# Where a per-head normalisation is computed: moving the retention norm from GpSimd to VectorE, with its square root made by Newton steps, and a weight panel split in quarters

## The reference

```python
def retention(rq, rk, rv, rg, cos, sin):
    ...  # o: per head, (q k^T * decay) v with causal exponential decay
    mu = jnp.mean(o, axis=-1, keepdims=True)
    var = jnp.mean(jnp.square(o - mu), axis=-1, keepdims=True)
    o = ((o - mu) * lax.rsqrt(var + GROUPNORM_EPS)).reshape(B, S, H * DV)
    return (o * jax.nn.silu(rg.astype(jnp.float32))).astype(rq.dtype)

for l in range(DEPTH_2):
    ...
    a = mla_attention(...)          # 8 heads, softmax attention
    r = retention(...)              # 8 heads
    mixed = jnp.concatenate([rmsnorm_2(a, beta_attn[l]), r * beta_ret[l]], axis=-1)
    x = x + mixed @ w_o[l]
    h = rmsnorm_2(x, mlp_norm[l])
    x = x + jnp.square(jax.nn.relu(h @ w_up[l])) @ w_down[l]
```

## Time and profile before

| what | us |
|---|---|
| median of 3 runs | 3416.02 |
| lowest and highest of the 3 | 3414.8 and 3417.39 |
| the profiled execution's own time | 3417.14 |
| its span | 3415.2 |
| PE busy in the span | 3308.8 |
| DVE, ACT, POOL busy | 1870.1, 1443.7, 323.3 |

### The profile page before, as it was taken

One profiled execution on the slowest core, in us unless ns is written; L12 is line 12 of the kernel. 1 busy time (PEld: TensorE's weight loads), 2 busy tenths in 40 slices (PEclk: granted clock), 3 DMA queues, 4 the chain that ended last, 5 costly groups with the idle time before them and its releaser, 6 DMA issues.

```text
span 3415.2 us, 45463 instructions
## 1 busy us (share of the span) xinstructions
PE 3308.8 (97%) x17167; PEld 2818.1 (83%) x17167; DVE 1870.1 (55%) x1978; ACT 1443.7 (42%) x1539; POOL 323.3 (9%) x272
## 2 busy tenths in 40 slices
PE   6999999999999899999999999999998999999998
PEld 6988788888888788778888888878877888888886
DVE  5877565555444544655555544454465555554444
ACT  5335453344344443544433444443354444334343
POOL 5332010000000101510000000000052000000000
PEclk9999999999999999999999999999999999999999
DMA  6444556555555455435665555555543555655553
GB/s 189 148 126 149 185 180 188 184 184 194 189 195 196 148 191 175 134 111 177 190 187 184 186 195 196 189 181 187 182 144 99 185 186 185 192 187 193 189 195 135
DMA packets 216948, 598.48 MB, mean 175 GB/s; under 512 B 16136, under 2 KB 57320, under 8 KB 183032
## 3 DMA queue, kind: packets, MB, share of 16 engines
q1 hardware_dynamic: 215528, 589.58, 53.0%
q0 software_dynamic: 1312, 7.41, 0.6%
HBM read 594.86 MB, written 2.10 MB: 175 GB/s over the span
## 4 chain that ended last, share of the span: by engine, by line
PE 90%; DVE 4%; issue 2%; ACT 2%; POOL 1%; DVEq 1%; POOLq 1%; ACTq 0%
PE ps L511 43%; PE ps L576 21%; PE ps L580 10%; PE ps L1137 5%; PE ps L926 3%; DVE wlo L1792 2%; PE ps L647 1%; PE ps L648 1%; PE ps L649 1%; ACT whi L1207 1%; PE ps L1076 0%; PE ps L1077 0%; PE ps L541 0%; PE ps L1106 0%; DVEq L1856 0%
## 5 line engine op out<-in xcount | busy, mean ns | idle before, releaser
L1792 DVE TENSOR_TENSOR wlo<-raw,whi 128x2048 fp32r<-128x2048 f32 (+2 forms) x547 | 1254.5, 2293 | 1277.3 <-ACT whi L1207 1276.2
L1207 ACT CAST whi<-raw 128x2048 fp32r<-128x2048 f32 (+2 forms) x552 | 1034.4, 1874 | 1530.8 <-PE ps L511 869.7
L576 PE MATMUL ps<-xT,whi 128*128 128x512 f32 x3072 | 840.2, 395 | 0.9 <-DVE xT L1818 0.9
L511 PE MATMUL ps<-whi,stage 128*128 128x512 f32 x3168 | 785.4, 389 | 2.9 <-DVE wlo L1792 2.4
L511 PEld LDWEIGHTS ps<-whi,stage 128*128 128x128 f32 x3168 | 594.1, 188 | 127.9 <-DVE wlo L1792 3.9
L576 PEld LDWEIGHTS ps<-xT,whi 128*128 128x128 f32 x3072 | 525.5, 189 | 72.2 <-DVE xT L1818 1.4
L580 PEld LDWEIGHTS ps<-xT,wlo 128*128 128x128 f32 x3072 | 472.1, 189 | 65.7
L580 PE MATMUL ps<-xT,wlo 128*128 128x256 f32 x3072 | 489.1, 281 | 0.0
L511 PE MATMUL ps<-wlo,stage 128*128 128x512 f32 x1584 | 424.1, 389 | 0.0
L511 PEld LDWEIGHTS ps<-wlo,stage 128*128 128x128 f32 x1584 | 297.4, 188 | 61.7
L511 PE MATMUL ps<-whi,xT 128*128 128x512 f32 x1344 | 336.3, 385 | 11.5 <-DVE wlo L1792 6.5
(11 more groups left out here) (423 smaller groups left out, 2401.9 us busy)
## 6 DMA issues: line engine op xcount, KB each, us to landing
raw<-in_mlp_w SPq DMA_DIRECT2D x128, 1024.0 KB, 5.1
raw<-in_w_up SPq DMA_DIRECT2D x128, 1024.0 KB, 5.3
raw<-in_w_down SPq DMA_DIRECT2D x128, 1024.0 KB, 4.9
raw<-in_w_in SPq DMA_DIRECT2D x100, 1024.0 KB, 5.2
raw<-in_w_o SPq DMA_DIRECT2D x32, 1024.0 KB, 5.2
raw<-in_w_out SPq DMA_DIRECT2D x16, 1024.0 KB, 5.2
raw<-in_w_in SPq DMA_DIRECT2D x16, 832.0 KB, 4.5
raw<-in_w_uq SPq DMA_DIRECT2D x8, 768.0 KB, 4.2
```

What stands on the lines that cost most here:

```text
L511: last = mm(psum(bank, width), x_of(part, r), w[:, s, at + c0:at + c0 + width], start=start and part == 0 and w is whi, stop=stop and part ...
L576: mm(psum(bank + j), whi[:, u % 2, c:c + P], xT[:, k, :], start=k == 0, stop=False)
L1207: act.copy(whi[:, u % 2, 0:width], raw[:, u, 0:width]).then_inc(sig["hi"], 1)
L1792: tt(wlo[:, u % 2, 0:width], raw[:, u, 0:width], whi[:, u % 2, 0:width].bitcast(F32), SUB).then_inc(sig["lo"], 1)
```

## The change

ACT no longer makes the root: DVE computes it at step 10 (`inverse_roots`) from an integer seed and three Newton steps, 12 small instructions with a drain between each two. DVE then normalises one pair of heads per step at steps 11 to 14 (`normalise`), in four instructions of 128 x 128. POOL waits for each pair (`nrm`) and only gates. The transposes of the pairs, their high parts and their low parts come one step later. The decays of heads 0 and 1 are made ahead, between the Silu and the cast of w_ukv's first panel. The cast of w_o's panel 0 becomes four parts of 512 columns at ACT's steps 2 to 5, its split four parts at DVE's steps 6 to 9; the cast of panel 1 four parts at ACT's steps 14 to 17. DVE's split of panel 1 moves from step 15 to step 18 and that of panel 2 from step 19 to step 20, both whole.

```diff
 PE, steps
-                    if 12 <= step < 16:
-                        retention_transposes(step - 12)
+                    if 13 <= step < 17:
+                        retention_transposes(step - 13)
 ACT, helper
+            def split_part(Q, u, c):
+                if c == 0:
+                    act.wait_ge(sig[f"raw{u}"], 16 * (Q + 1))
+                    act.wait_ge(sig["pan"], 4 * Q + u - 1)
+                part = act.copy(whi[:, u % 2, 512 * c:512 * c + 512], raw[:, u, 512 * c:512 * c + 512])
+                if c == 3:
+                    part.then_inc(sig["hi"], 1)
 ACT, behind the Silu
+                decays(0)
+                decays(1)
 ACT, steps
-                    if 1 <= step < 9:
+                    if 3 <= step < 9:
                         decays(step - 1)
                     if 2 <= step < 10:
                         retention_out(step - 2)
-                    if step == 5:
-                        split(w_o["quad"], 0, D)
-                    if step == 10:
-                        act.wait_ge(sig["gn"], at["gn"] + 1)
-                        fn(gstat[:, 2, :], moments[:, :, 1], ACT.Sqrt, bias=eps).then_inc(sig["gsq"], 1)
-                    if 13 <= step < 17:
-                        retention_hi(step - 13)
+                    if 2 <= step < 6:
+                        split_part(w_o["quad"], 0, step - 2)
+                    if 14 <= step < 18:
+                        retention_hi(step - 14)
                     if 10 <= step < 18:
                         softmax(step - 2)
-                    if step == 14:
-                        split(w_o["quad"], 1, D)
+                    if 14 <= step < 18:
+                        split_part(w_o["quad"], 1, step - 14)
 DVE, new
+                def inverse_roots():
+                    v, t, y = gstat[:, 0, :], gstat[:, 1, :], gstat[:, 2, :]
+                    ts(v, moments[:, :, 1], EPS, None, ADD)
+                    dve.drain()
+                    ts(y.bitcast(I32), v.bitcast(I32), 1, None, ALU.logical_shift_right)
+                    dve.drain()
+                    ts(y.bitcast(I32), y.bitcast(I32), -1, ROOT_SEED, MUL, ADD)
+                    for _ in range(3):
+                        dve.drain()
+                        tt(t, y, y, MUL)
+                        dve.drain()
+                        stt(t, t, -0.5, v, MUL, MUL)
+                        dve.drain()
+                        stt(y, t, 1.5, y, ADD, MUL)
+                    dve.drain()
+                def normalise(p):
+                    for h in (2 * p, 2 * p + 1):
+                        for r in range(RT):
+                            y, i = proj[:, r, C_RQ + h * P:C_RQ + (h + 1) * P], 8 * r + h
+                            last = ts(y, y, moments[:, i, 0:1], gstat[:, 2, i:i + 1], SUB, MUL)
+                    last.then_inc(sig["nrm"], 1)
 DVE, steps
-                        moments_of(7).then_inc(sig["gn"], 1)
+                        moments_of(7)
                     if 1 <= step < 17:
                         scores(step - 1)
                     if 3 <= step < 10:
                         moments_of(step - 3)
-                    if step == 6:
-                        split(w_o["quad"], 0, D)
+                    if 6 <= step < 10:
+                        split_part(w_o["quad"], 0, step - 6)
                     if step == 10:
-                        dve.wait_ge(sig["gsq"], at["gsq"] + 1)
-                        dve.reciprocal(gstat[:, 2, :], gstat[:, 2, :]).then_inc(sig["grc"], 1)
+                        inverse_roots()
+                    if 11 <= step < 15:
+                        normalise(step - 11)
                     if 11 <= step < 19:
                         weights(step - 3)
-                    if 13 <= step < 17:
-                        retention_lo(step - 13)
-                    if step == 15:
+                    if 14 <= step < 18:
+                        retention_lo(step - 14)
+                    if step == 18:
                         split(w_o["quad"], 1, D)
-                    if step == 19:
+                    if step == 20:
                         split(w_o["quad"], 2, D)
 POOL
-                    pool.wait_ge(sig["grc"], heads["grc"] + 1)
-                    ...
                     for p in range(4):
-                        ...
-                        pool.drain()
+                        pool.wait_ge(sig["nrm"], heads["nrm"] + p + 1)
                         c = slice(C_RQ + 2 * p * P, C_RQ + 2 * (p + 1) * P)
                         g = slice(C_RG + 2 * p * P, C_RG + 2 * (p + 1) * P)
                         tt(proj[:, :, c], proj[:, :, c], proj[:, :, g], MUL).then_inc(sig["ret"], 1)
```

More of the change, by code:

```diff
@@ L42 @@
 ROUND = 1.5 * 2.0 ** 23
+ROOT_SEED = 0x5f3759df
 W_IN1 = 4620
@@ L121 @@
     heads=dict(tT=16, evT=16, sc=16, wr=8, dS=16, nb=8, pr=8, xp=8, pt=8, vv=16, oo=8, om=8,
-               gn=1, gsq=1, grc=1, ret=4, rtr=4, rhi=4, rlo=4),
+               nrm=4, ret=4, rtr=4, rhi=4, rlo=4),
     mixed=dict(mx=1, mla=1, tr=4, trhi=4, xt=4), w_o=dict(quad=4),
@@ L333, in build @@
                  "evD", "evT", "fe", "fin", "fl", "fmix", "fn", "fp", "fsc", "ft", "fv", "fx", "g1", "g2",
-                 "g3", "g4", "g5", "gel", "gn", "gsh", "gst", "hi", "hn", "ld_cst", "ld_dt", "dtr", "ld_gain", "ld_gb",
+                 "g3", "g4", "g5", "gel", "nrm", "gsh", "gst", "hi", "hn", "ld_cst", "ld_dt", "dtr", "ld_gain", "ld_gb",
                  "ld_pos", "ld_pw", "ld_rows", "ld_ssm", "ld_x", "ld_xm", "ld_xr", "lo", "mix", "mlx", "msc", "g3f", "fxs", "fxl", "pxs", "pxl", "sxs", "sxl", "mxs", "mxl",
@@ L338, in build @@
                  "tT", "tr", "trhi", "upd", "uph", "vev", "vtr", "vv", "om", "rtr", "rhi", "rlo", "wm", "wr", "xn", "xp",
-                 "xt", "gsq", "grc", "ret", "mla", "half", "rsr", "tile", "sq", "ssum", "yps", "yst", "yt", "prm_c", "s5rot", "yev", "ld_x1", "ld_cst2", "evG", "ld_rows2", "zeros", "cpy2", "rawh0", "rawh1", "rawh2", "rawh3", "xmn", "mo0", "resid0", "zb", "zs"]
+                 "xt", "ret", "mla", "half", "rsr", "tile", "sq", "ssum", "yps", "yst", "yt", "prm_c", "s5rot", "yev", "ld_x1", "ld_cst2", "evG", "ld_rows2", "zeros", "cpy2", "rawh0", "rawh1", "rawh2", "rawh3", "xmn", "mo0", "resid0", "zb", "zs"]
         sig = {n: ctx.enter_context(nc.semaphore(n)) for n in names}
@@ L1648, in _, with decays @@
                     fn(proj[:, r, C_RG:W_IN2], proj[:, r, C_RG:W_IN2], ACT.Silu)
+                at = st.peek("heads")
+                def decays(i):
+                    if i >= 2:
+                        act.wait_ge(sig["dS"], at["dS"] + i - 1)
+                    fn(decay[:, i % 2, :], const("rel"), ACT.Exp, scale=LOG_GAMMA[i]).then_inc(sig["wr"], 1)
+                decays(0)
+                decays(1)
                 def q_rows():
@@ L1682, in transposed @@
                     last.then_inc(sig["evT"], 1)
[L1684 to L1687, removed]
                 def softmax(i):
@@ L1787, in _, with split_part @@
             MUL, ADD, SUB = ALU.mult, ALU.add, ALU.subtract
+            def split_part(Q, u, c):
+                if c == 0:
+                    dve.wait_ge(sig["hi"], 4 * Q + u + 1)
+                columns = slice(512 * c, 512 * c + 512)
+                part = tt(wlo[:, u % 2, columns], raw[:, u, columns], whi[:, u % 2, columns].bitcast(F32), SUB)
+                if c == 3:
+                    part.then_inc(sig["lo"], 1)
             def split(Q, u, width):
@@ L2457, in moments_of @@
                     for r in range(RT):
-                        last = dve.bn_aggr(moments[:, 8 * r + h, :], stats6[:, r, :])
+                        dve.bn_aggr(moments[:, 8 * r + h, :], stats6[:, r, :])
                     dve.drain()
-                    return last
+                def inverse_roots():
[19 more added lines that the diff above has]
+                    last.then_inc(sig["nrm"], 1)
                 def retention_lo(p):
@@ L2743, in _ @@
                     last.then_inc(sig["rope"], 1)
-                    pool.wait_ge(sig["grc"], heads["grc"] + 1)
-                    for r in range(RT):
-                        y = proj[:, r, C_RQ:C_RQ + 2 * P].rearrange("p (h n) -> p h n", h=2)
-                        tt(y, y, moments[:, 8 * r:8 * r + 2, 0:1].to_broadcast([P, 2, P]), SUB)
-                    pool.drain()
-                    for p in range(4):
[L2752 to L2759, removed]
+                    for p in range(4):
+                        pool.wait_ge(sig["nrm"], heads["nrm"] + p + 1)
                         c = slice(C_RQ + 2 * p * P, C_RQ + 2 * (p + 1) * P)
```

## The result

The changed kernel takes 3422.94 us (median of 20 runs, 3418.64 to 3427.64) against 3415.64 for the kernel before (20 runs, 3412.91 to 3417.54): ratio 1.0022, 95% interval 1.0015 to 1.0029. It is slower by 7.3 us; the interval does not hold 1. The profiled execution took 3419.29, span 3417.5, the third fastest of the twenty; the profiled execution of before took 3417.14. So the two traces differ by 2.15 us only, and not by 7.3.

The account below looks back on a forecast made before the run. PE, busy 97% of the span, bounds the kernel; its heads-stage gaps end on DVE and ACT. Per layer -6.85 + 2.5 + 0.3 + 5.1 = +1.05, so 3419.2 for one execution, median 3418.1; predicted 3418, range 3408.5 to 3424.

Parts of the forecast that it names:

- little changes: Forecast case: two to four slow-clock stretches in a layer, 3413.9 to 3419.9 us; chance 0.57.
- POOL's work bound nothing: Heads stage: no long PE gap ends on POOL, 8.4 us of slack, so moving the norm wins nothing by itself.
- Decays ahead, -0.15: Before w_ukv's first panel PE loses 0.85; before head 0's values 1.0 comes back; net -0.15 us.
- Quarters, -2.5 in a layer: Retention steps: PE's stalls on panel 0's whole cast and whole split go, gaining 1.0 + 1.5 us.
- Normalisation, 0.75 for a pair: DVE steps 11 to 14: 0.19 us per 128x128 operation from SBUF, 0.75 for a pair (0.36 to 1.2).
- DVE's walk to item 8's weights: DVE's scores, moments, root and pair 0 put the weights at 50.3; PE's gap grows from 1.58 to 4.1 us.
- The loop behind it: Steps 14 to 16: PE waits for DVE's scores, weights and low part, 2.97 us; step 18 starts at 77.6.
- The split of panel 1, +2.5 and panel 2, +0.3: Moved DVE splits, steps 18 and 20: PE waits +2.5 us for panel 1 and +0.3 for panel 2.
- The clock, 3.4 stretches of 1.5: Heads stage: PE's clock falls after 3.4 of five gaps in a layer, 1.5 us each, +5.1 in all.
- The clock that falls after every gap: Rival: five slow stretches in a layer, +3.45 us, giving 3422.9 us; chance 0.11.
- The port rival: DVE's steps 12 to 15: POOL gates of all four pairs meet small DVE operations, 0.9 each, 3423.5 us; chance 0.07.
- The clock that stays up: Rival: denser PE work leaves none or one slow stretch in a layer, 3407.9 to 3410.9 us; chance 0.20.

Follow-up runs that it names:

- norm_on_pool: The changed kernel with the root back on ACT and DVE and subtraction and multiplication back on POOL, all else kept: 3414.26 us.
- quarters_filled: The kernel before with only w_o's panel 0 cast and split in quarters, plus unread identity transposes in four of PE's gaps: 3406.28 us.
- quarters_only: The kernel before with only w_o's panel 0 cast in quarters at ACT's steps 2 to 5 and split at DVE's 6 to 9: 3409.06 us.
- norm_and_splits_back: The changed kernel with root and norm, and the splits of panels 1 and 2, back as before: 3409.30 us.
- newton_1: The changed kernel with one Newton step for the root instead of three, six small dependent operations fewer: 3416.96 us.

## Why the prediction was right or wrong

The time lies in the range (3408.5 to 3424), but 4.9 us over the 3418 named and 3 us over the range of the likeliest case (3413.9 to 3419.9). That case, little changes, is just missed: the middle of 1.0015 to 1.0029 lies over 0.2%. Which way each part pushes was right. From the runs, for both layers: quarters -5.4, decays ahead and later pairs about nothing, splits moved +5.0, root and norm +8.7. These four lead from the kernel before to the changed one, each kernel with one part more, so that they add up to the measured difference (8.3 against 7.3, for 1.1 us between the sets) is no check of them. What checks them are the runs that take the same part from another kernel: 6.4 for root and norm, 4.0 for the splits.

**POOL's work bound nothing**: right for this change. Taking 25.9 us from POOL won nothing, and putting it back (norm_on_pool) cost nothing that shows. The 8.4 us of slack are the last pair's; the first pair had 1.3, and in a stage as dense as quarters_filled PE waits for it.

**Decays ahead, -0.15**: right. The wait is 1.03; behind it head 0's scores start 0.78 later than before once the drift is off (0.85 reckoned), and head 0's values 0.24 early.

**Quarters, -2.5 in a layer**: right in size; head 6's values at 36.5 after the drift, 36.6 foretold, and 2.7 in the run. They fit on both engines: a quarter cast took 0.62, a quarter split 0.69 (0.61 to the next start). The 2.7 is in part another thing, the collision beside POOL's last gate, which the quarters end.

**Root, 3.0 us**: right, 3.13 from 1445.71 to the next scores, in which 0.22 is issue.

**Normalisation, 0.75 for a pair**: wrong, the term was mis-sized. It took 1.03 (1450.26 to 1451.29), 0.26 an operation. I interpolated from a 1024-wide one; the row from PSUM, 0.30, was the better measure. The Trainium skill (VectorE: DVE Perf Modes, the errata on SBUF sources) says that an operation which reads SBUF pays a fixed extra time, so that short ones suffer most. The trace agrees that a short operation is mostly fixed time: 128 columns take 0.26, and an eighth of the 0.71 of 1024 columns is 0.09. It does not show that the source matters: two operations of that width from PSUM stand 0.26 apart as well (1459.78 to 1460.30). Such a pair stands twice on the path, 0.6 in a layer.

**DVE's walk to item 8's weights, PE resuming at 50.35**: 51.5 after the drift, 1.1 late. 0.28 is the norm; the rest are mostly issue pauses of 0.2 to 0.4 at three places that I had left out. The gap is 5.2, not 4.1.

**The loop behind it**: the mechanism was right, three waits on L2505, with step 14 longest. Step 18 starts at 82.4 after the drift (1483.00), 4.8 later than the 77.6 reckoned at full clock. The slow stretches below hold 3.0 to 3.2 of that, so the walk itself was 1.6 to 1.8 too short, 1.1 of it before item 8's weights.

**Root and norm together**: this is the part that was mis-sized most. The prediction's step 18, 77.6 at full clock, is 2.4 under the 84.47 less its three slow stretches (4.5). In that are 2.65 of quarters and decays and 0.9 of the collision, so 1.2 in a layer was left for root and norm: 2.4 for both layers, 3.6 with the 0.6 of clock added to each. The runs gave 8.7 and 6.4. The 1.6 to 1.8 by which the walk was too short bring 3.6 to about 7.

**The split of panel 1, +2.5 and panel 2, +0.3**: 2.24 before panel 1 in the trace, and 4.0 to 5.0 us for both layers against 5.6 in the runs. Right in size.

**The clock, 3.4 stretches of 1.5**: that it falls behind gaps is shown; how often and for how long was not foretold. In the profiled execution it fell behind the two longest gaps of each layer, 5.2 and 2.8, and not behind the other three. PE's passes stood 0.21 apart and not 0.11 for 3.2 us each time in the first layer, for 5.6 and 5.8 in the second: 3.2 and 5.7 us of PE's time, against the 5.1 reckoned for each. By the stretches, the clock missing from full is 3.3 us in the first layer (15 x 0.11 + 18 x 0.09) and 6.9 in the second (15 x 0.23 + 19 x 0.18), before 5.1 in either (15 x 0.11 + 18 x 0.19, 15 x 0.14 + 19 x 0.16; the 4.5 of the prediction was low). So the two traces have the same slow clock, 10.1 and 10.2 us.

**The forecast for one execution, 3419.2 against 3419.29**: in part luck. PE's transposes of the attention output start 1.5 us later than before in the first layer (1498.62 against 1497.11, 0.9 without the drift), and 3.35 more in the second: 4.3 in the two stages where I had reckoned 2.1. Behind them, where nothing was changed, this execution gains 2.6 on that of before: PE's last products start at 3402.73 against 3400.42.

**The median, put 1.12 under that execution**: it lies 3.65 over it, so 3418.1 for the median was 4.8 short although the forecast for one execution was met. The changed kernel's executions spread over 9.0 us, those of the kernel before over 4.6, in twenty runs each. The mean granted clock goes with the time: the three at 0.988 took 3426.4 on average, the five at 0.991 3419.7 (the correlation over twenty is -0.84), and the profiled execution is one of the 0.991. That points at more slow clock in the median execution than in the one with a trace, but no trace shows it.

**How much of the loss is the clock's.** Filling the gaps took 6.1 us away, but a kernel with norm and splits in their old place gains by it too. With both unfilled the changed kernel lies 13.9 over quarters_only, with both filled 10.5 (3416.80 against 3406.28). So some 3 us are the clock's, with an uncertainty as large, and most of the loss stays when the clock stays up: it is DVE's path to the weights and to panel 1.

**The rivals.** The clock that falls after every gap had the measured time, 3422.9, but by luck: in no trace did it fall behind each gap, and the walk was 1.7 too short as well. The port rival did not come: in the changed kernel's trace no gate meets the small L2459, which took 0.17 each time. What it rests on is real: in norm_and_splits_back's second layer the same operation started 0.09 behind a gate (2571.72 and 2571.63) and took 1.20. ACT's quarters fitted. The clock that stays up came true only where the gaps were filled.

**What stays open**: how many slow stretches the median run has in each layer and how long they are, since only one execution has a trace, and how the -3 beyond the six operations in newton_1 divides between clock and chance.

## What to carry to other kernels

Before work moves off an engine, ask whether any wait ends on it, at the first pair as well as at the last: here none did, and the engine that got the work had no time to spare at the place where it got it. A chain of tiny dependent operations costs its count (0.25 each at 128x16), so don't put it before something for which another engine waits. Cutting a long operation into the slots of a pipeline's loop is worth it where the long one stands in the way (5.4 us here for two layers); moving a long one to the end, right before its consumer, is not (4.0 to 5.0 us lost). Where PE waits a few us again and again, unread transposes that fit inside the gap can win as much as a better order (6.1, 4.35 and perhaps 2.8 us in three kernels), as the granted clock then stays at 2.4 GHz.

## What the runs showed of the hardware that I had not expected

Tensor-scalar operations of 128x128 fp32 start 0.26 us apart on DVE, from SBUF to SBUF (a row of four) as from PSUM (a row of two). With 79 more PE passes a layer in its gaps the changed kernel got 6.1 us faster, and the standard deviation of its runs fell from 2.6 to 1.4 us. Executions of one and the same kernel differ by 9 us, more than the change is worth, and the slower ones have the lower mean granted clock (0.988 to 0.991).
